# Two transformer blocks on one core: grouped norm factors, silu units inside the attention, an earlier norm and aligned buffers in block two

## The reference

```python
h = _rmsnorm(x, norm_g[l])
z = h @ w_in[l]
(nsa_q, nsa_kv, nsa_gate, nsa_silu, fox_qkv, fox_f, fox_silu, mem_q, mem_silu, merge_g) = _split(z, IN_SPLITS)
o_a = _nsa(...) * jax.nn.silu(nsa_silu)      # q, k: rmsnorm per head of 64, then rope; three attentions
o_b = _fox(...) * jax.nn.silu(fox_silu)      # q, k: rmsnorm per head; logits + cumulated log-forget
mem_kv = _rmsnorm(mem, mem_norm_g[l]) @ w_mem_kv[l]
o_m = _memory_xattn(...) * jax.nn.silu(mem_silu)   # 4 heads of 128, 256 memory tokens
g = jax.nn.sigmoid(merge_g)
u = g[0] * (o_a @ w_branch_a) + g[1] * (o_b @ w_branch_b) + g[2] * (o_m @ w_branch_m)
x = x + u @ w_out[l]
```

## Time and profile before

| | us |
|---|---|
| median of 3 runs | 3395.55 (3387.1 to 3395.87) |
| the profiled execution | 3397.67 |
| its span | 3396.2 |
| PE busy | 3167.8 (93%) |
| GpSimd busy | 1887.5 (56%) |
| DVE busy | 1667.0 (49%) |
| ACT busy | 792.0 (23%) |

### The profile page before, as it was taken

How to read it: one execution, slowest core, us unless ns; L and a number is a source line. 1 busy time by engine, 2 the same in 40 slices (tenths; PEclk the granted TensorE clock), 3 DMA queues, 4 the chain that set the end, 5 groups by cost and what they waited for, 6 DMA issues and landing times.

```text
span 3396.2 us, 42398 instructions
## 1 busy us (share of the span) xinstructions
PE 3167.8 (93%) x15474; PEld 2586.2 (76%) x15474; DVE 1667.0 (49%) x3712; ACT 792.0 (23%) x1755; POOL 1887.5 (56%) x2174
## 2 busy tenths in 40 slices
PE   7999999899998989999978799999998889999999
PEld 6777777788887767888767677788887767778887
DVE  2333334466503756663056666653225766665232
ACT  1111111222201422221021116641002112663100
POOL 5555553599974775998723550047774454005775
PEclk9999999899998999999978899999998888999999
DMA  3222221222222221222321220012223121001222
GB/s 138 89 88 83 98 87 45 67 93 93 95 98 68 73 83 62 94 94 99 101 104 44 75 69 1 1 44 99 94 94 117 50 73 58 2 1 59 97 94 86
DMA packets 66445, 255.74 MB, mean 75 GB/s; under 512 B 7616, under 2 KB 8128, under 8 KB 64320
## 3 DMA queue, kind: packets, MB, share of 16 engines
q1 hardware_dynamic: 62496, 227.57, 20.0%
q10 hardware_dynamic: 3744, 25.47, 2.0%
HBM read 250.91 MB, written 2.10 MB: 74 GB/s over the span
## 4 chain that ended last, share of the span: by engine, by line
PE 87%; DVE 8%; issue 2%; ACT 2%; DMA 0%; POOL 0%; ACTq 0%; DVEq 0%; POOLq 0%
PE bank L331 21%; PE bank L332 21%; PE bank L333 21%; PE bank L1559 4%; PE bank L1536 3%; PE bank L1549 2%; PE bank L369 2%; PE bank L359 1%; PE bank L593 1%; PE bank L361 1%; PE bank L360 1%; PE bank L1531 1%; PE bank L1109 1%; PE bank L565 1%; PE bank L581 1%
## 5 line engine op out<-in xcount | busy, mean ns | idle before, releaser
L1846 POOL TENSOR_TENSOR w_lo<-w_raw,w_hi 128x256 fp32r<-128x256 f32 x1736 | 1409.5, 842 | 36.2
L1842 POOL TENSOR_SCALAR w_hi<-w_raw 128x1024 fp32r<-128x1024 f32 x434 | 479.0, 1104 | 1452.5 <-PE bank L333 1222.3
L331 PE MATMUL bank<-in_hi,w_hi 128*128 128x512 f32 x1408 | 568.0, 403 | 5.3 <-ACT factor_wide L422 2.8
L332 PE MATMUL bank<-in_lo,w_hi 128*128 128x512 f32 x1408 | 561.6, 399 | 0.0
L333 PE MATMUL bank<-in_hi,w_lo 128*128 128x512 f32 x1408 | 561.0, 398 | 0.0
L331 PE MATMUL bank<-z_hi,w_hi 128*128 128x512 f32 x976 | 398.9, 409 | 1.6 <-DVE silu L1684 1.6
L332 PE MATMUL bank<-z_lo,w_hi 128*128 128x512 f32 x976 | 392.2, 402 | 0.0
L333 PE MATMUL bank<-z_hi,w_lo 128*128 128x512 f32 x976 | 390.9, 400 | 0.0
L331 PEld LDWEIGHTS bank<-in_hi,w_hi 128*128 128x128 f32 x1408 | 267.8, 190 | 67.9 <-ACT factor_wide L422 3.5
L333 PEld LDWEIGHTS bank<-in_hi,w_lo 128*128 128x128 f32 x1408 | 267.5, 190 | 64.7
L332 PEld LDWEIGHTS bank<-in_lo,w_hi 128*128 128x128 f32 x1408 | 267.8, 190 | 61.3
(11 more groups left out here) (398 smaller groups left out, 5305.2 us busy)
## 6 DMA issues: line engine op xcount, KB each, us to landing
w_raw<-in_units SPq DMA_DIRECT2D x434, 512.0 KB, 3.4
bias<-in_bias ACTq DMA_DIRECT2D x8, 1152.0 KB, 5.1
o_all<-in_cmp_w ACTq DMA_DIRECT2D x4, 2048.0 KB, 8.5
x_res<-in_x ACTq DMA_DIRECT2D x4, 512.0 KB, 9.0
mem_in<-in_mem ACTq DMA_DIRECT2D x2, 1024.0 KB, 4.8
out<-x_res ACTq DMA_DIRECT2D x1, 2048.0 KB, 6.3
consts<-in_consts ACTq DMA_DIRECT2D x1, 710.5 KB, 3.8
both_layers_cols<-in_layer_cols ACTq DMA_DIRECT2D x2, 140.5 KB, 4.1
```

Of the source, the lines that this page charges most:

```text
L331: pe.matmul(out, hi[:, w], rh, start=start and n == 0, stop=False)
L332: pe.matmul(out, hi[:, w], rl, start=False, stop=False)
L1842: d = c.s.unit_hi.on(pool.tensor_scalar(c.w_hi[s][:, :], c.w_raw[s][:, :], 1.0, 0.0, ALU.mult, ALU.add))
L1846: last = pool.tensor_tensor(c.w_lo[s][:, w], c.w_raw[s][:, w], c.w_hi[s][:, w].bitcast(F32), ALU.subtract)
```

## The change

- `Area.take`: buffers of 512 bytes and more start at a multiple of 512; the layout of block two is made anew.
- Start: the norm of block two's first layer takes its chunks one by one as the residual of the last feed-forward layer comes (`dve_norm_start` as elsewhere); constants and masks are loaded and cast at the end of that feed-forward layer. The norm of the second layer is made chunk by chunk behind the residual adds of the first layer's w_out, with eight buffers for the squares.
- Projections: order of units changed (sel_k, win_k before nsa_q), four banks instead of three. Five groups of q/k units share one factor chain each (on up to 48 columns); ACT widens. nsa_q and mem_q are not multiplied by their factor: it becomes the scale of the exponent, and PE doesn't spread it. The gain goes into ACT's copy. The forget rows of all eight heads are made in advance.
- Attention: one pipeline of 144 tasks, without staging (the logits take 64 partitions of q and k); each silu unit is given to PE in eight pieces of three matmuls, one a step, into bank 7; turning back, Silu, gating and the split of chunk n-1 run inside chunk n. The first six merge gate units fill the tail.
- End: x is stored in four DMAs of two chunks each.

```diff
@@ Area.take @@
-        t = self.nc.alloc_sbuf_tensor_at(name, shape, dt, offset=self.at)
-        size = 1
+        size = 2 if dt == BF16 else 4
         for n in shape[1:]:
             size *= n
-        self.at += -(-size * (2 if dt == BF16 else 4) // 32) * 32
+        step = 512 if size >= 512 else 32
+        self.at = -(-self.at // step) * step
+        t = self.nc.alloc_sbuf_tensor_at(name, shape, dt, offset=self.at)
+        self.at += -(-size // 32) * 32
...
+    if layer == 1:
+        act.wait_ge(*c.s.lo_done["hid", layer, FC - 1])
+        c.s.consts_loaded.on(act.dma_start(c.kk[:, :], c.t["consts"]), "consts", 16)
+        for k in range(2):
+            c.s.consts_loaded.on(act.dma_start(c.cols[:, k, :], c.t["layer_cols"][k]), ("cols", k), 16)
...
+        self.w, self.last, self.col = self.heads * self.tiles, which[-1], col
+        self.cols = self.w * len(which)
+        self.r = c.group_r[col // 64][:, 0:self.cols]
+        for i, s in enumerate(self.of):
+            s.group, s.at = self, i * self.w
...
+    out += [("k", c.sel_k[:, :], G_SEL_K), ("k", c.win_k[:, :], G_WIN_K)]
+    out += [("q", c.nsa_q[:, n, :], G_NSA_Q) for n in range(4)]
...
+    groups = [Group(c, which, out, 64 * i) for i, which in
+              enumerate(([3, 4, 5, 6, 7, 8], [11, 12, 14, 15], [13, 16, 19, 22], [23, 24, 25, 26], [27, 28, 29, 30]))]
...
+SPREAD = {10: 3, 11: 4, 17: 11, 18: 12, 19: 14, 20: 15, 28: 23, 29: 24, 30: 25, 31: 26, 32: 27, 33: 28, 34: 29, 35: 30}
+ROPE = {1: 0, 11: 3, 12: 4, 13: 5, 14: 6, 15: 7, 16: 8}
+SLOTS_TWO = 35
...
+def later(every, groups, m):
+    s = every[m - 1] if 1 <= m <= SLOTS_TWO else None
+    if s and s.kind in ("q", "k"):
+        yield "sums", s
+    if m in groups:
+        yield "factors", groups[m]
+    if m in SPREAD:
+        yield "spread", every[SPREAD[m]]
+    if m in ROPE:
+        yield "rope", every[ROPE[m]]
+    if s and s.kind == "rows":
+        yield "turn", s
+    if s and s.kind == "gates":
+        yield "gates", s
...
+    elif what == "factors":
+        c.free[7] = c.s.sums_read[layer, s.last]
     elif what == "spread":
-        pe.wait_ge(*c.s.factor_found["ep", layer, s.m])
-        if s.heads == 2:
-            pe.wait_ge(*c.s.prepared["wide", layer, s.m])
...
+def act_widen(act, c, layer, s):
+    act.wait_ge(*c.s.factor_found["ep", layer, s.group.last])
+    if s.m >= 25:
+        act.wait_ge(*c.s.factor_spread["ep", layer, s.m - 2])
+    r = s.group.r[:, s.at:s.at + s.group.w]
+    c.s.widened.on(act.activation(c.ep_wide[s.m % 2][:, :].rearrange("p (h d) -> p h d", d=HD), r.unsqueeze(2).to_broadcast([P, 2 * s.tiles, HD]), ACT.Copy), (layer, s.m))
...
+def dve_group_factors(dve, c, layer, g, z):
+    step, count = c.s.dve_step, len(g.of)
+    dve.wait_ge(*c.s.tokens_summed["ep", layer, g.last])
+    dve.wait_ge(*c.s.prepared[z.name])
+    def split(ap):
+        return ap.rearrange("p (s w) -> p s w", w=g.w)
+    f, f2 = (a.unsqueeze(1).to_broadcast([P, count, g.w]) for a in z.head_factor(g.heads))
+    m, a, r = c.group_m[:, 0:g.cols], c.group_a[:, 0:g.cols], g.r
+    d = c.s.sums_read.on(dve.scalar_tensor_tensor(split(m), split(c.bank[7][:, g.col:g.col + g.cols]), g.heads / P, f2, ALU.mult, ALU.mult), (layer, g.last))
+    dve.wait_ge(*d)
+    d = step.on(dve.tensor_scalar(m, m, EPS, None, ALU.add))
+    dve.wait_ge(*d)
+    d = step.on(dve.tensor_scalar(a.bitcast(I32), m.bitcast(I32), 1, None, ALU.logical_shift_right))
+    dve.wait_ge(*d)
+    d = step.on(dve.tensor_scalar(r.bitcast(I32), a.bitcast(I32), -1.0, float(0x5F3759DF), ALU.mult, ALU.add))
+    for _ in range(3):
+        dve.wait_ge(*d)
+        d = step.on(dve.tensor_tensor(a, r, r, ALU.mult))
+        dve.wait_ge(*d)
+        d = step.on(dve.scalar_tensor_tensor(a, a, -0.5, m, ALU.mult, ALU.mult))
+        dve.wait_ge(*d)
+        d = step.on(dve.scalar_tensor_tensor(r, a, 1.5, r, ALU.add, ALU.mult))
+    dve.wait_ge(*d)
+    d = c.s.factor_found.on(dve.tensor_tensor(split(r), split(r), f, ALU.mult), ("ep", layer, g.last))
+    if g.last == 8:
+        dve.wait_ge(*d)
+        dve.tensor_scalar(c.nsa_scale[:, :], r[:, 2 * g.w:], HD ** -0.5, None, ALU.mult)
+        step.on(dve.tensor_scalar(c.nsa_minus[:, :], r[:, 2 * g.w:], -HD ** -0.5, None, ALU.mult), ("nsa_scale", layer))
+    if g.last == 22:
+        dve.wait_ge(*d)
+        dve.tensor_scalar(c.mem_scale[:, :], r, P ** -0.5, None, ALU.mult)
+        step.on(dve.tensor_scalar(c.mem_minus[:, :], r, -P ** -0.5, None, ALU.mult), ("mem_scale", layer))
...
+CHUNK, TASKS = 36, 144
+GATE_STEPS = {s: (0, s - 10) for s in range(10, 18)} | {s: (1, s - 19) for s in range(19, 27)} | {s: (2, s - 28) for s in range(28, 36)}
+GATE_OUT = {18: (0, 0), 27: (0, 1), 0: (1, 2)}
+BACK = {5: 0, 7: 1, 9: 2}
+BACK_HI, BACK_LO = {6: 0, 8: 1, 10: 2}, {7: 0, 9: 1, 11: 2}
+TAIL_MERGE = {144: (0, 1), 145: (1, 2), 146: (2, 0), 147: (3, 3), 148: (4, 4)}
...
+    z, tasks = c.layer_norm(layer), tasks_of(layer)
+    pe.wait_ge(*c.s.roped[layer, 8])
+    pe.wait_ge(*c.s.stored["cmp", layer])
+    for now in range(STEPS):
+        if now < TASKS:
+            pe_logits(pe, c, tasks[now])
+        if 0 <= now - 2 < TASKS:
+            pe_turn(pe, c, tasks[now - 2])
+        if 0 <= now - 4 < TASKS:
+            pe_output(pe, c, tasks[now - 4])
+        n, step = divmod(now, CHUNK)
+        if n < 4 and step in GATE_STEPS:
+            u, k = GATE_STEPS[step]
+            pe_silu_tile(pe, c, layer, z, 3 * n + u, k)
+        if n and step in BACK:
+            pe_back(pe, c, layer, n - 1, BACK[step], 6 if now == TASKS + 7 else 7)
+        if now in TAIL_MERGE:
+            j, b = TAIL_MERGE[now]
+            pe_merge_unit(pe, c, layer, z, 0, j)
+        if now == TASKS + 7:
+            pe_merge_unit(pe, c, layer, z, 0, 5)
...
+        pe.matmul(b[:, 0:NC], c.nsa_q[h, t.n, q], c.cmp_k[h, :], start=True, stop=False)
...
+        if n and step == 3:
+            act_silu(act, c, layer, n - 1)
+        if n and step in BACK_HI:
+            j = BACK_HI[step]
+            act.wait_ge(*c.s.gated["back", layer, n - 1, j])
+            c.s.hi_done.on(act.activation(c.o_hi[j][:, n - 1, :], c.o_all[:, n - 1 + 4 * j, :], ACT.Copy), ("back", layer, n - 1, j))
...
+def act_silu(act, c, layer, n):
+    for j in range(3):
+        act.wait_ge(*c.s.evicted["silu", layer, 3 * n + j])
+        s = c.o_all[:, n + 4 * j, :]
+        c.s.act_step.on(act.activation(s, s, ACT.Silu), ("silu", layer, n, j))
...
+def exp_scale(c, t):
+    if t.kind == "fox":
+        return HD ** -0.5
+    col = t.n * TT + t.i if t.kind == "mem" else (t.n * TT + t.i) * 2 + t.j
+    return (c.mem_scale if t.kind == "mem" else c.nsa_scale)[:, col:col + 1]
...
+        z = c.layer_norm(1)
+        act.wait_ge(*c.s.unit_multiplied["branch", 0, 3, 2])
+        c.s.w1_loaded.on(act.dma_start(c.w1, c.t["cmp_w1"][2]), (1, 0), 16)
+        for k in range(DC):
+            act.wait_ge(*c.s.residual_added["w_out", 0, k])
+            act_norm_chunk(act, c, z, k)
+    else:
+        for k in range(1, DC, 2):
+            act.wait_ge(*c.s.residual_added["w_out", 1, k])
+            c.s.out_stored.on(act.dma_start(c.t["out"][:, (k - 1) * T:(k + 1) * T], c.x[:, k - 1:k + 1, :].rearrange("p a b -> p (a b)")), k, 16)
...
```

More of the change, by code:

```diff
@@ L1058, in layer_begins @@
-def layer_begins(c, layer):
-    return c.s.residual_added["w_out", layer - 1, DC - 1] if layer else c.s.prepared["layer", 0]
-def same_turn(every, s, back, heads=None):
-    for x in every:
-        if x.kind == s.kind and x.turn == s.turn - back and heads in (None, x.heads):
-            return x
-    return None
-def last_wide(every, s):
-    found = [x for x in every if x.kind == "norm" and x.heads == 2 and x.turn < s.turn and x.turn % 2 == s.turn % 2]
-    return found[-1] if found else None
+    for i, s in enumerate([s for s in out if s.kind in ("q", "k")]):
+        s.turn = i
@@ new lines, in later, with two_turns_back @@
+def later(every, groups, m):
[12 more added lines that the diff above has]
+        yield "gates", s
+def two_turns_back(every, s):
+    kinds = ("rows",) if s.kind == "rows" else ("q", "k")
+    return [x for x in every if x.kind in kinds and x.turn == s.turn - 2][0]
@@ new lines, in pe_silu_tile @@
+def pe_silu_tile(pe, c, layer, z, u, k):
+    key = ("silu", layer, u)
+    assert c.order[c.u] == key
+    if k == 0:
+        pe.wait_ge(*c.s.unit_split[c.u])
+        pe_free(pe, c, 7)
+    hi, lo, w, out = c.w_hi[c.u % SLOTS], c.w_lo[c.u % SLOTS], slice(k * P, k * P + P), c.bank[7][:, :]
+    pe.matmul(out, hi[:, w], z.hi[:, k, :], start=k == 0, stop=False)
+    pe.matmul(out, hi[:, w], z.lo[:, k, :], start=False, stop=False)
+    last = pe.matmul(out, lo[:, w], z.hi[:, k, :], start=False, stop=k == DC - 1)
+    if k == DC - 1:
+        pe_unit_done(c, key, last)
+        c.free[7] = c.s.evicted["silu", layer, u]
@@ L1521, in pe_logits, with pe_back @@
+def pe_back(pe, c, layer, n, j, b):
+    pe.wait_ge(*c.s.stored["rows", layer, n, j])
+    pe_free(pe, c, b)
```

(11 more changed lines are left out.)

622 lines of the change are left out of this document (292 added, 330 removed).

## The result

The changed kernel takes 3433.48 us (median, 3431.46 to 3437.23) beside 3395.71 for the kernel before: ratio 1.0119, 95% interval 1.0104 to 1.0134. It is 38 us slower, where 3230 us was forecast. Outside attention 150 us of gain arrived, where 145 was forecast; attention, where 22 more was forecast, lost 184.

The account below looks back on a forecast made before the run. PE was taken as the bound: its instructions at their pitch, its waits and its half-clock stretches. Gains 38 + 11 + 9 + 3 + 84 + 22 = 167 us from 3397.7 gave 3230 us, range 3110 to 3300.

Parts of the forecast that it names:

- Silu bursts: Attention: ScalarE's Silu between Exps needs table loads and makes PE wait, 2.3 us each for three, 7 a layer (0 to 18).
- Rival D: Attention: DVE becomes the bound, its short instructions slowed beside GpSimd; 3440 us at the extreme, chance 0.04.
- Alignment: fp32r matmuls: moving operands at multiples of 512 bytes bring the pitch to 226.6 ns; 38 us gain.
- Rival B: fp32r matmuls: pitch doesn't follow alignment, and weights aligned alike may even meet the moving tile; 3268 us, chance 0.12.
- Rival A: All fp32r matmuls: a multiple of 512 does more than 128, pitch 215 ns; another 116 us, 3114, chance 0.15.
- Start of layer 0: Block two's first norm: a chunked start cuts PE's wait of 15.22 us before its first z matmul; 11 us gain.
- Layer 1: Start of the second layer: each z chunk made right behind its residual chunk, 33.9 us down to 25; 9 us gain.
- End: Final store of x: pairs stored as they come replace one 2 MB store of 6.3 us; 3 us gain.
- Projections: Projections of both layers: 5 factor chains replace 22, reducing idle PE and clock loss; 42 us a layer, 84 gain.
- rival C: Projections and attention: DVE and its chains stay the bound, 44 us less and 22 less gain; 3296 us, chance 0.18.
- Attention and silu: Attention with silu units: one pipeline recovers 23 us of loss, less 15 new, plus 3 from keys; 11 us a layer.
- cold start: Start of attention, PE busy at clock 0.50 in a window; 11 us a layer counted as loss to recover.

Follow-up runs that it names:

- no_silu_table: The kernel after with ACT.Copy in place of ACT.Silu on the gate tiles, so the gate is not applied as it should be: 3309.61 us, ratio 0.9759.
- before_aligned: The kernel before with SBUF tiles of 512 bytes and more beginning at multiples of 128 bytes: 3388.06 us beside 3389.19, ratio 0.9997.
- full_rows: The kernel after with cmp, sel, win and fox logits contracting all 128 rows, summing both heads, so computed otherwise: 3237.81 us, ratio 0.9558.
- padded: The kernel after with VectorE staging the second head's q and zeroing it in place, so logits contract 128 rows, same result: 3249.81 us, ratio 0.9586.
- padded_no_table: padded with Copy in place of Silu on the gate tiles, so the gate is not applied as it should be: 3222.28 us, ratio 0.9501.
- before_half: The kernel before with its logits reading the head's 64 rows of q and keys in place of the padded halves: 3611.57 us, ratio 1.065.
- padded_exp_gate: padded with the gate as x/(1+exp(-x)): exp(-x) on ScalarE from the table held, add, reciprocal and multiply on VectorE: 3236.06 us, ratio 0.956.

## Why the forecast was wrong

**The step that failed** is one clause: "Half-partition stationaries replace the zeroed halves: same columns, taken at no change". It priced a matmul by its columns, and no row of the trace of before had a 64-row matmul followed by a 128-row one. It should have been bounded from both sides like the other unseen costs; the range had no room for it, and none of the rivals was it. It cost 92 + 2 us a layer: 69 by the clock, 25 by the changes of row count. The part of the clock needs the waits too: without the Silu bursts, no_silu_table, attention is 58 us a layer shorter with the same 64 rows (350.8 for 409.0), where the bursts cost 16 with 128 rows. Rival D, the one on the slow side, named another mechanism, DVE, and a time near the truth, 3440. DVE is busy 161 of 372 us and PE's waits for it are small: D didn't happen, the number is chance.

**Alignment**: 38 forecast, 33 measured by itself (27 to 39). Size right by luck, reason wrong: the residue of the moving operand modulo 128 alone gives nothing (before_aligned), and the change gained only because it puts both operands at multiples of 512. Rival B feared in passing that the weights "may even meet the moving tile" and so cost time; their address does matter, but being alike is what was quick. Rival A (215 ns) didn't come: nothing at a multiple of 512 is under 226.

**Start of layer 0**: 11 forecast; PE's wait went from 15.22 to 4.19 us. The whole way to the spread is 15.3 shorter. **Layer 1**: 9 forecast, 8.1 measured, with the same 2.07 us wait for the factor. **End**: 3 forecast, 3.7. **Projections**: 84 forecast, 47.1 + 43.5 = 90.6; rival C fell.

**Attention and silu**: 11 gain a layer forecast, with 7 for the Silu bursts. full_rows, which has all of the change but the 64 rows, gains 2.0 us a layer (315.0 for 317.0): 9 less. The bursts cost 16 where I had 7 (padded less padded_no_table; 12.5 if full_rows is set against padded_no_table), which covers 5.5 to 9 of it: I had counted PE's waits and not the slow clock behind each, which I did count in the projections. The 11 for the cold start was not in its row either: 12 us at half clock lose 6, the whole 17 lose 8.5. "ScalarE: Activation LUTs" of the Trainium skill (section "What ACT_TABLE_LOAD costs"), weighed in the forecast, asks for 1.38 us more at each load. The loads read here show none: at 2038.79 one runs 1.28 us and the Exp follows 0.01 us later.

With 128-row logits the sum stands: full_rows 3238 and padded 3250 us against the 3230 forecast for the whole.

## What to carry to other kernels

Don't price a matmul by its columns alone: one that contracts half of the rows cost more here than one with zeroed halves, 0.2 to 0.3 us each, and many times that when the clock is down. Where some must stay, try to bring full-row matmuls close behind the places where PE waits; an order of tasks was worth 110 us here. Begin the moving and the stationary operand at the same residue modulo 256 bytes; both at multiples of 512, or 384 with 128, are the pairs measured. And when a change replaces one form of an instruction by a form that the trace of before doesn't contain, bound it, however harmless it looks.

## What the runs showed of the hardware

- With 64-row matmuls every few microseconds, TensorE was busy throughout and at 1.2 GHz for 40 us (clock 0.50, 39.66 of 40.00 us busy), 80 us in before_half. With the same matmuls it held 2.4 GHz for 260 us (no_silu_table). In the returns shown, 128-row matmuls came right before. The page "TensorE: Matmul & The Clock Gate" of the Trainium skill (section "Why this matters for your kernels") advises to keep TensorE busy without a break to reach full clock; in these 40 us it was, and did not.
- Zeros in half of the rows leave the clock alone: padded has 0.96 from first logits to first branch, as full_rows.
- All 128 rows don't rule it out: the kernel before was busy 16.96 of 17.00 us at 0.50 at its attention's start.
- Same residue modulo 256 bytes of both operands (pairs 0 and 0, 384 and 128 modulo 512): 226 to 228 ns for 512 columns in fp32r, in the other pairs seen 232 to 234.
- DVE's reciprocal of fp32 takes 0.94 us for 128 columns (padded_exp_gate) and 3.35 for 512 (on 64 partitions, kernel after).
